# Small products of a three-layer kernel issued side by side, and the sums of its norms taken one step earlier

## The reference, cut to what matters

```python
# first block, per layer: indexer scores choose keys for attention "a" (8 heads of 64), "b" is differential (4 heads x 2 x 64)
rel = relu(einsum('bthd,bsd->bths', qi, ki)); iscore = einsum('bths,bth->bts', rel, wi)
o_a = softmax(qa @ k_sel * scale) @ v_sel
o_b = (softmax(q1 @ k1) - lam * softmax(q2 @ k2)) @ vb
h = h + token_mixers(rms_norm(h, g)); h = h + conv_ffn(rms_norm(h, g)); h = h + gate(rms_norm(h, g)) * (p @ w)
# second block: chunked attention "c" (8 heads of 64), and a recurrence over 8 heads of 64
def step(state, inp):
    sa = einsum("bhij,bhj->bhi", state, at)
    state = state * wt + sa[..., None] * bt + vt[..., None] * kt
    return state, einsum("bhij,bhj->bhi", state, rt)
# then a router with 32 experts, a gate, and layer norms between them
```

## Time and profile before

| | us |
|---|---|
| median of 3 runs | 3105.61 (3098.68 to 3106.81) |
| profiled execution | 3098.97 |
| its span in the profile | 3097.5 |
| mean granted TensorE clock | 0.942 of full |
| TensorE busy | 2842.3 (92%) |
| VectorE busy | 1674.8 (54%) |
| ScalarE busy | 1230.0 (40%) |

### The profile page before, as it was taken

One profiled execution on the slowest core, in us unless ns is written; L12 is line 12 of the kernel. 1 busy time (PEld: TensorE's weight loads), 2 busy tenths in 40 slices (PEclk: granted clock), 3 DMA queues, 4 the chain that ended last, 5 costly groups with the idle time before them and its releaser, 6 DMA issues.

```text
span 3097.5 us, 36057 instructions
## 1 busy us (share of the span) xinstructions
PE 2842.3 (92%) x14676; PEld 2102.9 (68%) x14676; DVE 1674.8 (54%) x2758; ACT 1230.0 (40%) x1793; POOL 119.5 (4%) x101
## 2 busy tenths in 40 slices
PE   6989999999999998999999998998989889679986
PEld 5766677888877776667788875856667658344445
DVE  4596445545445487445646455344433525477767
ACT  2217643423343216642424233244222322267665
POOL 0010000000000010000000000000000000022210
PEclk9999999999999899999999998989989889789998
DMA  3111222222222111223222221302111023379992
GB/s 116 65 55 67 73 106 89 96 95 95 92 85 69 57 69 62 75 80 118 82 95 96 95 82 68 124 24 77 42 44 52 35 90 135 151 260 392 372 347 95
DMA packets 64137, 334.90 MB, mean 108 GB/s; under 512 B 9568, under 2 KB 10336, under 8 KB 31072
## 3 DMA queue, kind: packets, MB, share of 16 engines
q1 hardware_dynamic: 58848, 324.14, 29.0%
q0 software_dynamic: 5120, 8.40, 0.9%
HBM read 312.58 MB, written 28.31 MB: 110 GB/s over the span
## 4 chain that ended last, share of the span: by engine, by line
PE 77%; DVE 12%; ACT 5%; DMA 3%; issue 2%; SPq 0%; POOL 0%; POOLq 0%; DVEq 0%; ACTq 0%
PE bank L873 14%; PE bank L875 14%; PE bank L874 14%; PE bank L1036 3%; PE bank L1079 2%; PE bank L1109 2%; PE bank L1038 2%; PE bank L1037 2%; PE bank L2931 2%; PE bank L2212 2%; ACT wh L1805 1%; DVE wl L1274 1%; PE bank L2917 1%; DMA arena<-in_WE 1%; PE bank L2918 1%
## 5 line engine op out<-in xcount | busy, mean ns | idle before, releaser
L873 PE MATMUL bank<-XH,wh 128*128 128x512 f32 x1344 | 542.8, 404 | 21.0 <-DVE XL L1315 16.9
L874 PE MATMUL bank<-XL,wh 128*128 128x512 f32 x1344 | 531.8, 396 | 0.0
L875 PE MATMUL bank<-XH,wl 128*128 128x512 f32 x1344 | 531.4, 395 | 0.0
L1274 DVE TENSOR_TENSOR wl<-raw,wh 128x2048 fp32r<-128x2048 f32 (+1 forms) x168 | 371.8, 2215 | 225.9 <-ACT wh L1805 225.7
L1805 ACT ACTIVATE wh<-raw 128x2048 fp32r<-128x2048 f32 (+1 forms) x168 | 308.9, 1841 | 189.0 <-DMA raw<-in_W 186.7
L873 PEld LDWEIGHTS bank<-XH,wh 128*128 128x128 f32 x1344 | 257.0, 191 | 105.9 <-issue 26.0
L875 PEld LDWEIGHTS bank<-XH,wl 128*128 128x128 f32 x1344 | 257.4, 192 | 55.4
L874 PEld LDWEIGHTS bank<-XL,wh 128*128 128x128 f32 x1344 | 257.8, 192 | 52.4 <-issue 1.9
L873 PE MATMUL bank<-arena_rounded,wh 128*128 128x512 f32 x576 | 230.5, 400 | 5.3 <-DVE arena_rounded L1519 3.2
L874 PE MATMUL bank<-arena_rounded,wh 128*128 128x512 f32 x576 | 229.0, 398 | 0.0
L875 PE MATMUL bank<-arena_rounded,wl 128*128 128x512 f32 x576 | 228.9, 397 | 0.0
(11 more groups left out here) (477 smaller groups left out, 4703.6 us busy)
## 6 DMA issues: line engine op xcount, KB each, us to landing
raw<-in_W SPq DMA_DIRECT2D x153, 1024.0 KB, 4.9
arena<-in_WE SPq DMA_DIRECT2D x56, 1024.0 KB
hT<-in_WE SPq DMA_DIRECT2D x26, 1024.0 KB, 10.0
cst<-in_WE SPq DMA_DIRECT2D x14, 1024.0 KB, 9.8
gsave<-scr SPq DMA_DIRECT2D x48, 256.0 KB, 2.4
scr<-gsave SPq DMA_DIRECT2D x48, 256.0 KB, 4.0
raw<-in_W SPq DMA_DIRECT2D x8, 768.0 KB, 4.3
arena<-ytok SPq DMA_DIRECT2D x8, 512.0 KB, 7.1
```

The costliest lines, as they stand in the source:

```text
L873: pe.matmul(ps[0:c.stop - c.start, :], h[:, k, c], hi, start=i == 0, stop=False)
L874: pe.matmul(ps[0:c.stop - c.start, :], h[:, k, c], lo, start=False, stop=False)
L875: mm = pe.matmul(ps[0:c.stop - c.start, :], l[:, k, c], hi, start=False, stop=i == len(xs) - 1)
L1274: w_lo.inc(dve.tensor_tensor(wl[:, i % 3, 0:k], raw[:, i % 3, 0:k], wh[:, i % 3, 0:k].bitcast(F32), ALU.subtract), i)
```

## The change

1. **Recurrence, preparation.** The copies with zeroed rows are gone: `Bt` and `Kt` are written once, by two VectorE products. X0, LR and MK are made from 64 rows of contraction and 64 output rows each, in a quarter of the array; head 0 goes to one bank and head 1 to another, so X0 needs two banks and is read by two VectorE instructions of half the width. LR0 and LR1 are now the heads and no longer the halves of the chunks.
2. **Recurrence, scan.** The update of the state is four products of 64 x 64 x 64 (two heads, two terms) and no longer two of 64 x 128 x 128.
3. **Attention.** In kinds a and c the products of queries and keys of two heads are issued next to each other in even steps, and the two products with values, interleaved, in odd steps. They now stand ahead of the "turn" of their step. In kind b both banks are opened ahead of the first product.
4. **Indexer scores.** Two heads next to each other at the start of a step, in banks 7 and 6; bank 6 is shared with the rotations.
5. **Norms.** VectorE no longer adds the last tile: TensorE sums the partial sum over tiles 0 to 6 and then the last square (or the last tile of `hT`) into the same bank. ScalarE asks for the table of the root ahead of it. At the end of the feed-forward part the weight block's remainder comes after the last addition instead of before. The first two tiles of the feed-forward part are interleaved by k.

```diff
-                    for i in scores_at(s)[0:1]:
-                        score(i)
+                    if scores_at(s):
+                        two_scores(scores_at(s))
...
+        def products_at(jobs, s):
+            if s >= len(jobs):
+                return ()
+            if jobs[s][0] == "b":
+                return ((s, 0), (s, 1))
+            return ((s, 0), (s + 1, 0)) if jobs[s][2] % 2 == 0 else ()
+        def values_at(jobs, s):
+            if not 0 <= s - 3 < len(jobs):
+                return ()
+            if jobs[s - 3][0] == "b":
+                return (s - 3,)
+            return (s - 4, s - 3) if jobs[s - 3][2] % 2 else ()
...
+            def norm_sums(r):
+                key = ("sum", r)
+                ps = opened(key)
+                last, ready = (SQ[1], square((r, 7))) if r < 6 else (hT[:, 7, :], h_ready(r, 7))
+                for src, when in ((ACC, added((r, 6))), (last, ready)):
+                    pe.wait_ge(*when)
+                    for ti in range(4):
+                        mm = pe.matmul(ps[:, ti:ti + 1], src[:, tt(ti)], ones[:, 0:1], start=src is ACC and ti == 0,
+                                       stop=src is not ACC, skip_group_check=True)
+                bank.filled(mm, key)
...
+                        for i in done:
+                            pe.wait_ge(*bank.empty(("turn", m, i)))
+                        for j in range(ti + 1):
+                            for i in done:
+                                h = todo[i][2]
+                                r0 = 64 * (h % 2)
+                                v_ = wv[:, j, 0:64] if kind == "a" else vn[:, j, 64 * h:64 * h + 64]
+                                mm = pe.matmul(bank.ap(key)[r0:r0 + 64, tt(h // 2)], v_, PT[i % 2][:, tt(j)],
+                                               start=j == 0, stop=j == ti)
...
+                            if q == 0 and which == 0:
+                                two_tiles([("up", li, 0, 0, i) for i in range(2)], weights(n, 256), lambda k: x((3 * li + 1, k)))
...
-                        if k % 2:
+                        last = ci == 2 and k == 7
+                        if k % 2 and not last:
                             cuts_to(n + 2)
...
+            def root_table():
+                act.activation(tz(204), ones[:, 0:1], ACT.Sqrt)
...
-                for name, lhs in (("LR", p.Bz), ("MK", p.Kz)):
-                    for half in range(2):
-                        ps = opened((f"{name}{half}", j))
-                        for c in range(4 * half, 4 * half + 4):
-                            for h in range(2):
-                                mm = pe.matmul(ps[pr:pr + 64, col:col + 128], lhs[h][:, 64 * c:64 * c + 64],
-                                               p.AR[:, 128 * c:128 * c + 128], start=True, stop=True)
+                for name, lhs in (("LR", p.Bt), ("MK", p.Kt)):
+                    ps = [opened((f"{name}{h}", j)) for h in range(2)]
+                    for c in range(8):
+                        for h in range(2):
+                            pr, hr, col = 64 * (c % 2), 64 * h, 128 * (c // 2)
+                            mm = pe.matmul(ps[h][pr:pr + 64, col:col + 128], lhs[hr:hr + 64, 64 * c:64 * c + 64],
+                                           p.AR[hr:hr + 64, 128 * c:128 * c + 128], start=True, stop=True)
...
-                    pe.matmul(o, p.Bn[pr:pr + 64, 128 * cp:128 * cp + 128], u, start=True, stop=False)
-                    mm = pe.matmul(o, p.Kn[pr:pr + 64, 128 * cp:128 * cp + 128], vn_, start=False, stop=True)
+                    for lhs, rhs in ((p.Bn, u), (p.Kn, vn_)):
+                        for h in range(2):
+                            hr = 64 * h
+                            mm = pe.matmul(ps[hr:hr + 64, 256 + hr:320 + hr], lhs[pr:pr + 64, 128 * cp + hr:128 * cp + hr + 64],
+                                           rhs[:, hr:hr + 64], start=lhs is p.Bn, stop=lhs is p.Kn)
...
-                for src, dst in ((p.aT, p.Bz), (p.kT, p.Kz)):
-                    for h in range(2):
-                        ins = dve.scalar_tensor_tensor(out=dst[h], in0=src, scalar=hm[h], in1=E3, op0=ALU.mult, op1=ALU.mult)
-                pv.inc(ins, ("BK", j))
+                dve.tensor_tensor(p.Bt, p.aT, E3, ALU.mult)
+                pv.inc(dve.tensor_tensor(p.Kt, p.kT, E3, ALU.mult), ("BK", j))
```

More of the change, by code:

```diff
@@ L288, in plan_win @@
             for s in range(21):
+                for i in scores_at(s):
+                    bank.plan(("score", li, i), 7 - i % 2)
                 if s == 4:
@@ L313, in plan_win @@
                     bank.plan(("rot", li, t), 6)
-                for i in scores_at(s):
-                    bank.plan(("score", li, i), 7)
         def scores_at(s):
@@ L367, in plan_attention @@
             for s in range(len(jobs) + 6):
-                if s < len(jobs):
-                    for e in range(2 if jobs[s][0] == "b" else 1):
-                        bank.plan(("qk", m, s, e), 2 + n_s % 3)
-                        n_s += 1
+                for i, e in products_at(jobs, s):
+                    bank.plan(("qk", m, i, e), 2 + n_s % 3)
+                    n_s += 1
                 while 8 * g < pieces_by(m, s):
@@ L385, in plan_attention @@
                     n_p += 1
-                if 0 <= s - 3 < len(jobs) and jobs[s - 3][2] == 0:
-                    bank.plan(("acc", m, jobs[s - 3][0], jobs[s - 3][1]), 7)
+                if values_at(jobs, s) and jobs[values_at(jobs, s)[0]][2] == 0:
+                    kind, ti, _ = jobs[values_at(jobs, s)[0]]
+                    bank.plan(("acc", m, kind, ti), 7)
                 for d, name in ((4, "subsum"), (5, "subspread")):
@@ L544, in program @@
         square = Signal(sem("square"), [(r, k) for r in rms_at for k in range(8)])
-        added = Signal(sem("added"), [(r, k) for r in ALLN for k in range(1, 8)])
+        added = Signal(sem("added"), [(r, k) for r in ALLN for k in range(1, 7)])
         nroot = Signal(sem("nroot"), ALLN)
@@ L876, in tile, with two_tiles @@
                 bank.filled(mm, key)
+            def two_tiles(keys, w, fresh):
+                ps = [opened(key) for key in keys]
+                h, l = w
+                for k, hi, lo in xs:
+                    pe.wait_ge(*fresh(k))
+                    for i, key in enumerate(keys):
+                        c = slice(128 * i, 128 * i + 128)
+                        pe.matmul(ps[i], h[:, k, c], hi, start=k == 0, stop=False)
+                        pe.matmul(ps[i], h[:, k, c], lo, start=False, stop=False)
+                        mm = pe.matmul(ps[i], l[:, k, c], hi, start=False, stop=k == KT - 1)
+                        if k == KT - 1:
+                            bank.filled(mm, key)
             def weights(n, n_cols):
@@ L1009, in first_projections @@
                         rotate(li, t)
-                    for i in scores_at(s)[1:2]:
-                        score(i)
                     if t is not None:
@@ L1139, in ffn @@
                             split(n)
-                            for i in range(2):
-                                first = q == 0 and which == 0 and i == 0
-                                tile(("up", li, q, which, i), weights(n, 256), slice(128 * i, 128 * i + 128), xs,
-                                     (lambda k: x((3 * li + 1, k))) if first else None)
+                            if q == 0 and which == 0:
+                                two_tiles([("up", li, 0, 0, i) for i in range(2)], weights(n, 256), lambda k: x((3 * li + 1, k)))
+                            else:
+                                for i in range(2):
+                                    tile(("up", li, q, which, i), weights(n, 256), slice(128 * i, 128 * i + 128), xs)
                             n += 1
@@ L1660, in ple @@
                         add_to_norm(r, k - 1)
-                add_to_norm(r, 7)
             cuts_to(0)
             dve.wait_ge(s_in, 16)
-            for k in range(1, 8):
+            for k in range(1, 7):
                 add_to_norm(0, k)
@@ L2002, in ple @@
                         square_of(r, k - 1)
+                root_table()
                 square_of(r, 7)
@@ L2237, in prep @@
                 yield
-                ps = opened(("X0", j))
+                ps = [opened((f"X0{h}", j)) for h in range(2)]
                 pe.wait_ge(*pv(("BK", j)))
```

138 lines of the change are left out of this document (74 added, 64 removed).

## The result

| | before | after |
|---|---|---|
| median of 4 runs each, same chip | 3103.76 (3098.68 to 3106.81) | 3025.49 (3019.69 to 3027.41) |
| ratio | 1 | 0.9751 (95%: 0.9736 to 0.9766) |
| profiled execution | 3098.97 | 3027.41 |
| mean granted clock | 0.942 | 0.940 |

A forecast was written before the change was run, and what follows sets the result against it. TensorE, busy 92% of the span, was taken as the bound. Attention 6 + 14, recurrence 20, scores 12 and norms 7 sum to 59 us off 3098.97, giving 3040, stated as 3045 on the runs' median basis; range 3000 to 3082.

The forecast's parts named there:

- The gross gain: Attention: a pair of products costs what one costs, saving 68 us over three stretches, 22.7 in each, before losses.
- What comes back: Attention, kind a: longer TensorE waits at weight blocks and gates cost 13 us a layer, slower clock 6.6; net gain 3.
- the chain of 10.1 us: Attention: rounding, remainder, softmax work and gate with table loads before the values, 10.1 us; 6.2 left uncovered, wait becomes 4.
- In kind c 14 were forecast: Attention, kind c: 22.7 us gross less 6 waits and 2.5 clock, plus 2 clock back; 16, taken as 14.
- rival 1: Attention: waits stay covered and the clock holds; attention gives 50 to 68 us, total 89 to 107, 3000 to 3015; chance 0.17.
- The 2.2 us charged: Attention, kind a: half-rate clock behind each of three new waits in a layer, 2.2 us each, 6.6 in all.
- Recurrence: 20 forecast: Recurrence: shorter VectorE wait 5 us, LR and MK in quarters 5, state update about 10; sum 20, bounds 8 and 26.
- The update: Recurrence scan: eight small instructions take 0.28 us in place of 0.64, 11 us over 32 chunks, less 1.
- Rival 3: Recurrence: quarters don't run together and the update gains nothing; recurrence gives 8 us, total 3057; chance 0.05 by itself.
- Scores: 12 forecast: Indexer scores: a pair costs one, 8.7 us a layer, less 2.7 for bank 6 waits; net 6, 12 for both.
- Norms: 7 forecast: Norms: third norm 3.4 us a layer, interleaved tiles about 1 each, other norms nothing or small losses; sum 7.
- The likeliest case: Whole kernel: the forecast itself holds, 3020 to 3064 us; chance 0.48.

The follow-up runs named there:

- two_step_before: Also run 12: kernel before the change, with VectorE taking the remainder of kind a and c weight blocks one step after ScalarE's rounding; 3081.2 us, ratio 0.994.
- two_step_block: Also run 10: early_relu kernel, with VectorE taking the remainder of kind a and c weight blocks one step after ScalarE's rounding; 2977.9 us, ratio 0.9609.
- Runs 8: Changed kernel, with the weight blocks of kinds a and c taken whole one step later by both ScalarE and VectorE; 3032.1 us, ratio 0.9778.
- early_relu: Changed kernel, with ScalarE's relu of the odd score directly behind the even one at the start of its step; 3005.7 us, ratio 0.9702.
- the part alone: Kernel before the change, with only the recurrence's preparation and scan changes (items 1 and 2); 3081.9 us, ratio 0.9941.
- run 5: Kernel before the change, with only the recurrence's state update by heads, four small products for two; 3091.8 us, ratio 0.997.
- run 3: Kernel before the change, with only the indexer scores of two heads side by side and bank 6 shared; 3094.8 us, ratio 0.9981.
- Run 9: The early_relu kernel: changed kernel, with ScalarE's two relus together at the start of its step; 3005.7 us, ratio 0.9702.
- run 4: Kernel before the change, with only the norms' changes (item 5); 3099.4 us, ratio 0.9998.
- the parts alone: Four kernels, each the kernel before with one part only: attention 3066.5 us, recurrence 3081.9, scores 3094.8, norms 3099.4.
- the halves of the recurrence: Two kernels, each the kernel before with one half of the recurrence change: state update only, 3091.8 us; preparation only, 3087.9 us.

## Why the prediction was right, and where not

**Attention: the two large numbers were fair, their difference was not.** The gross gain was worked out as 22.7 us a layer. Between two_step_before and two_step_block, where neither waits nor clock are much in the way, TensorE's busy time in kind a goes from 119.2 to 97.8: 21.4. What comes back was put at 13 for waits and 6.6 for the clock. The waits grew by 8.8 us (7.7 to 16.5), because at the four blocks the values wait 2.0 to 2.9 us and not 4: the chain of 10.1 us has a gate and two table loads in it, and in the changed kernel ScalarE makes the copy that the values wait for first and takes the gate behind it (the copy at 351.97, the table load at 352.25). The waits that stood there already were misread too: of the 6.7 us only 3.0 were at blocks, and 3.04 were the spread of kind b's last norm, which stays (2.94 after). The clock of the stage went from 0.97 to 0.93: 6.8 us at half rate became 17.0. By the same halving that the prediction used that costs at most 5 us, and by my estimate 3 or more, since TensorE waits through part of these stretches. 22 less 9 less 3 to 5 is 8 to 10, and the stage shows 10.3 and 10.6. So the term that was mis-sized is what comes back in waits and clock in kind a, 20 us charged and 12 to 14 paid, in both layers; the mechanism itself, waits ahead of the values at each block and half rate behind some of them, is what the trace shows. In kind c 14 were forecast and 17.7 came, with waits 8 us longer (6 forecast).

What the prediction missed is that this price was not a property of pairing. Runs 8 and 10 show what the wait is made of: ScalarE's rounding (1.8 us) and VectorE's remainder (2.3 us) one after the other, with either engine's share of attention queued behind both. Taken whole a step later it only finds another victim; taken apart it nearly goes. And run 12 shows that the kernel before paid for it too, by 19 us. With the series broken in both, pairing is worth 122.2 - 103.4, 122.2 - 104.5 and 129.2 - 112.8, in sum 53 us, which is rival 1's lower end. The rival that the waits stay covered was false for this kernel and is true one edit away.

**The clock** was weighed against the Trainium skill's "TensorE: Matmul & The Clock Gate" (the table of why this matters), by which an idle stretch between bursts takes the array back to half rate. The trace agrees in kind: kind a went to 0.93 with 8.8 us more of waits, and to 0.98 and 1.00 when they were taken away. It also shows that the length of one wait doesn't decide by itself: in the changed kernel half rate stands behind the waits of 2.75 us (375.31) and 2.91 us (402.32), for 3.4 us each, and not behind that of 2.65 us (352.38). The 2.2 us charged for each of three new stretches was more than the 1.7 that 3.4 us at half rate can cost. In the first projections early_relu removed 6 us of waits and gained 15: more than half of it came by the clock.

**Recurrence: 20 forecast, 27 by stages, 18 by the median of the part alone.** The wait for VectorE ahead of X0 fell over the four preparations from 6.9 to 1.1 us (5 forecast). LR and MK fell by 1.74 us each time (1.3 forecast, the rest being held hidden behind VectorE). Some of the two did come back: waits for VectorE elsewhere in the stage grew by 3.3 us, so that its idle time fell by 2.5 only (45.1 to 42.6) while TensorE's busy time fell by 21.5. X0, forecast at 0, fell by 0.45: its 32 instructions were at 37 ns each, which I took as already the best, and are now at 23. The update fell by 0.26 us a chunk, not 0.34, since its eight new instructions take 0.38 and not the 0.28 of the row that I took: 8 us over 32, where I had 11. By the rows of one preparation that would be 4 x 3.9 + 8 = 24, less the 3.3 that came back; the rest of the 27 goes with a higher clock in the stage, 0.90 where the kernels with the old recurrence have 0.86 to 0.89. The strict form of the warning in "TensorEngine Tiling (Array Packing)" of the Trainium skill (Performance Considerations), that an already small dimension should not be shrunk, did not hold here: twice the instructions at half the columns took 0.38 us for 0.64, and run 5 agrees with 9 us. Rival 3 is out.

**Scores: 12 forecast, 7 by stages, 6 by run 3.** The pair does cost one. I had priced bank 6's waits at 2.7 us a layer; the rows show waits of 1.03, 0.17, 0.37, 1.59 and more, 5.7 us more idle time in the stage of the first layer (17.4 to 23.1, by windows over it), and a fall of the clock behind two of them, which I had not priced at all. Run 9 shows the cause: the odd relu at the end of ScalarE's step holds the bank. With it early the waits on a relu, 3.9 us in this stage, are gone.

**Norms: 7 forecast, 3 by stages, 1 by run 4.** The third norm gave 2.1 us in the first layer, not 3.4: the sums did start earlier, but 16 of them took 1.92 us at full rate where 8 had taken 1.84 at half rate, and the clock still fell behind them, for 3.4 us (6.8 before). The second norm lost 1 us, which I had at 0 (idle 2.27 to 1.48, sums 1.32 to 3.11).

The errors had both signs (attention +19, recurrence +7, scores -5, norms -4), and the median sits 20 us under the forecast, inside its range. The likeliest case held by its time. But attention gave nearly twice what was worked out for it, and the scores and norms about half or less, so that the total came as near as 20 us is in part luck.

**Still open:** why the parts alone add up to 58 us and together to 77; why unchanged code runs at different clocks from kernel to kernel (the old first projections of the second layer take 264.9 to 276.1 us at 0.91 to 0.95); and what is missing of the clock in the halves of the recurrence. It shifts the comparison of single profiles by some 5 us a stage, which is why means over several kernels were used.

## What to carry to other kernels

When a saved product shortens the cover of a long piece of side work, look at how that piece is built before charging the wait: two engines in series that both have a share in the critical loop can be put into different steps, and here that edit was worth some 28 us after the change and 19 before it. The wait next to a piece of side work is not its whole price: follow the chain to later waits, and read the granted clock of the stretch behind each (2.04 us of waiting had 17 us at half rate behind it). And where a bank is newly shared, move its reader up together with its writer.

## What the runs showed of the hardware

- Instructions with 64 rows of contraction and 64 output rows, taking the four quarters in turn, follow each other about twice as fast as the form with 128 rows of contraction: 61 of them with 128 columns in 1.91 us, 31 ns each, where that form took 59; and 29 with 64 columns in 0.66 us, 23 ns each, where it took 37.
- Kind a of the first layer: one wait of 3.04 us had 6.8 us at 1.2 GHz behind it (0.97 over the stage); with no wait above 1.6 us the clock was 1.00; with waits of 2.0 to 2.9 us there were four stretches at 1.2 GHz, 17 us in all (0.93), one of them behind waits of 0.78, 0.83 and 1.61 us close together.
- Kind c before: 17 us at 1.2 GHz behind a wait of 2.04 us, though TensorE was busy in all of it.
